# Two slots in place of three in the rings of rounded weight panels, each panel split one panel ahead

## The reference, cut to what matters

```python
# first_block, for each of 2 layers
y = rms_norm(x, in_norm_g) @ w_in + b_in          # then mLSTM, HGRN2 and a sliding-window attention
x = x + concat(m_out, h_out, s_out) @ w_out
x = x + square(relu(rms_norm(x, mlp_norm_g) @ w_up)) @ w_down          # width 4096
gate = sigmoid(rms_norm(x, ple_norm_g) @ w_ple_gate)
e = rms_norm(p @ w_ple_proj, ple_post_norm_g)
x = x + gate * e

# second_block, for each of 2 layers; mod is a product of the conditioning c
h = rmsnorm(x, g_attn) * (1 + scale1) + shift1
x = x + gate1 * mixer_layer(h)                    # w_in, three attentions, w_out
h = rmsnorm(x, g_mlp) * (1 + scale2) + shift2
u, g = split(h @ w_up)                            # width 2816 each
x = x + gate2 * ((silu(conv(g)) * u) @ w_down)
# after both: rmsnorm(x, g_final)
```

## Time and profile before

| what | value |
|---|---|
| median of 3 runs | 3312.72 us (3269.17 to 3331.93) |
| the profiled execution, its own time | 3291.14 us |
| its span, first to last instruction | 3289.3 us |
| its mean granted TensorE clock | 0.911 |
| TensorE busy | 2956.2 us, 90% of the span |
| TensorE weight loads busy | 2410.1 us, 73% |
| VectorE busy | 1736.4 us, 53% |
| ScalarE busy | 1126.6 us, 34% |
| remainders of panels (L308, VectorE) | 218 instructions, 469.5 us |
| roundings of panels (L296, ScalarE) | 218 instructions, 392.3 us |

### The profile page before, as it was taken

The page is one execution under the profiler, slowest core; times in us unless marked ns, Lnnn a source line. Parts: engine busy times, 40 slices in busy tenths (PEclk is TensorE's granted clock), DMA queues, the critical chain, the costliest instruction groups (busy, mean ns, idle before and its releaser), DMA issues. The chain is left out here.

```text
span 3289.3 us, 37690 instructions
## 1 busy us (share of the span) xinstructions
PE 2956.2 (90%) x14514; PEld 2410.1 (73%) x14514; DVE 1736.4 (53%) x2899; ACT 1126.6 (34%) x1851; POOL 197.9 (6%) x195
## 2 busy tenths in 40 slices
PE   5977889999879778899998699889999898989997
PEld 3957668888659576688886587768887687768886
DVE  4458356666654574555566554454352643454453
ACT  3251432222433515322234334433232434333232
POOL 1012010000200120100002000010001000010001
PEclk9955699999989558999999899999999899989999
DMA  4200024444132000244440311122321310122321
GB/s 162 98 13 1 1 70 160 167 168 154 69 116 90 13 1 14 91 160 164 161 166 32 129 64 32 35 77 87 112 82 53 125 63 28 44 73 77 120 87 61
DMA packets 42992, 281.35 MB, mean 86 GB/s; under 512 B 5944, under 2 KB 6200, under 8 KB 11704
## 3 DMA queue, kind: packets, MB, share of 16 engines
q1 hardware_dynamic: 42808, 278.86, 24.2%
HBM read 276.75 MB, written 2.10 MB: 85 GB/s over the span
## 5 line engine op out<-in xcount | busy, mean ns | idle before, releaser
L308 DVE TENSOR_TENSOR low_panels<-raw_panels,high_panels 128x2048 fp32r<-128x2048 f32 (+3 forms) x218 | 469.5, 2153 | 357.8 <-ACT high_panels L296 357.7
L296 ACT ACTIVATE high_panels<-raw_panels 128x2048 fp32r<-128x2048 f32 (+3 forms) x218 | 392.3, 1801 | 525.6 <-PE bank L1347 196.7
L409 PE MATMUL bank<-mlp_h_high,high_panels 128*128 128x512 f32 x1216 | 485.2, 399 | 37.8 <-DVE mlp_h_low L399 19.0
L409 PE MATMUL bank<-mlp_h_low,high_panels 128*128 128x512 f32 x1216 | 479.4, 394 | 0.0
L409 PE MATMUL bank<-mlp_h_high,low_panels 128*128 128x512 f32 x1216 | 479.2, 394 | 0.0
L409 PEld LDWEIGHTS bank<-mlp_h_high,high_panels 128*128 128x128 f32 x1216 | 230.1, 189 | 103.0 <-issue 36.8
L409 PEld LDWEIGHTS bank<-mlp_h_high,low_panels 128*128 128x128 f32 x1216 | 230.1, 189 | 51.6
L409 PEld LDWEIGHTS bank<-mlp_h_low,high_panels 128*128 128x128 f32 x1216 | 230.5, 190 | 48.1
L1347 PE MATMUL bank<-mlp_hid_high,high_panels 128*128 128x512 f32 x512 | 204.9, 400 | 0.0
L1347 PE MATMUL bank<-mlp_hid_low,high_panels 128*128 128x512 f32 x512 | 202.9, 396 | 0.0
L1347 PE MATMUL bank<-mlp_hid_high,low_panels 128*128 128x512 f32 x512 | 202.9, 396 | 0.0
(11 more groups left out here) (355 smaller groups left out, 5835.3 us busy)
## 6 DMA issues: line engine op xcount, KB each, us to landing
raw_panels<-in_w SPq DMA_DIRECT2D x238, 1024.0 KB, 4.9
raw_panels<-in_w SPq DMA_DIRECT2D x16, 384.0 KB, 3.2
raw_panels<-in_w SPq DMA_DIRECT2D x4, 960.0 KB, 4.6
raw_panels<-in_w SPq DMA_DIRECT2D x4, 768.0 KB, 4.1
row<-in_row SPq DMA_DIRECT2D x2, 1476.0 KB
x<-in_xT SPq DMA_DIRECT2D x1, 2048.0 KB, 7.5
raw_panels<-in_w SPq DMA_DIRECT2D x4, 512.0 KB, 7.6
mix<-in_rope SPq DMA_DIRECT2D x2, 1024.0 KB, 8.5
```

Source lines behind the costliest of these rows:

```text
L296: self.nc.scalar.activation(self.g.high[:, i % SPLIT, 0:raw.shape[1]], raw, ACT.Copy).then_inc(self.high_ready, 1)
L308: self.nc.vector.tensor_tensor(self.g.low[:, i % SPLIT, 0:w], raw, self.g.high[:, i % SPLIT, 0:w].bitcast(F32), ALU.subtract).then_inc(sel ...
L409: ins = nc.tensor.matmul(bank[:, :], w[a][:, k, c0:c0 + P], rhs[b][:, k0 + k, :], start=first and k == 0 and j == 0, stop=last and k == kt ...
```

## The change

`SPLIT` goes from 3 to 2 and `AHEAD` from 2 to 1. The second split inside the norm is taken out of the two input stages, since the panel loop that follows now begins with panel 1. In `embedding_gate` the list is written anew: panel first + 1, the first gate panel, is now split there and no longer at the end of the MLP, and the panels after it two output chunks later than their predecessors were.

```diff
-SPLIT = 3
-AHEAD = 2
+SPLIT = 2
+AHEAD = 1
...
-                    norm_scalar(nc, act, g, e, hh, before={0: lambda: pan.high(act, 0), 3: lambda: pan.high(act, 1)})
+                    norm_scalar(nc, act, g, e, hh, before={0: lambda: pan.high(act, 0)})
...
-                                before={1: lambda: pan.low(dve, 0), 4: lambda: pan.low(dve, 1)})
+                                before={1: lambda: pan.low(dve, 0)})
...
-                pan.high(act, first + 2)
-                pan.high(act, first + 3, full, DC)
+                pan.high(act, first + 1)
                 for c in range(DC):
-                    if c == 2:
-                        pan.high(act, first + 4, full, DC + 2)
+                    if c in (0, 2, 4):
+                        pan.high(act, first + 2 + c // 2, full, DC + c)
                     act.wait_ge(full, DC + c + 1)
...
                 norm_vector(nc, dve, g, e, x, vec[:, V_GPLE:V_GPLE + DC], hh, hl, before={0: p_low})
+                pan.low(dve, first + 1)
                 pan.low(dve, first + 2)
                 dve.wait_ge(ee.root_ready, 1)
                 st.link(nc.vector.reciprocal(erstd[:, 1, :], erstd[:, 0, :]))
-                pan.low(dve, first + 3)
                 for c in range(DC):
-                    if c == 2:
-                        pan.low(dve, first + 4)
+                    if c in (2, 4):
+                        pan.low(dve, first + 2 + c // 2)
...
-                norm_scalar(nc, act, g, e, hh, mod[:, 0:DC], {0: lambda: pan.high(act, 0), 3: lambda: pan.high(act, 1)}, s("shifts_ready"))
+                norm_scalar(nc, act, g, e, hh, mod[:, 0:DC], {0: lambda: pan.high(act, 0)}, s("shifts_ready"))
...
-                            {1: lambda: pan.low(dve, 0), 4: lambda: pan.low(dve, 1)})
+                            {1: lambda: pan.low(dve, 0)})
```

## The result

| | before | after |
|---|---|---|
| median | 3309.98 us (20 runs, 3269.17 to 3332.68) | 3330.61 us (20 runs, 3308.64 to 3351.05) |
| ratio, 95% interval | | 1.0109 (1.0087 to 1.0130) |
| profiled execution: time, span, granted clock | 3291.14 us, 3289.3 us, 0.911 | 3331.29 us, 3329.5 us, 0.903 |

The kernel is slower, by less than 2%. The ratio sets aside eight of the 20 runs of the kernel before, those over 1.5% above its fastest, and none of the kernel after, so it stands above the 1.0062 of the two medians (20.6 us).

A forecast was written before the change was run, and what follows sets the result against it. TensorE, busy 90% of the span, was taken as the bound, with splits hidden over long stretches. Terms summing to +25.0 us on a base of 3301.9 gave 3327 us, 0.75% slower, range 3283 to 3368.

The forecast's parts named there:

- the two bases: Starting times for the forecast: the profiled execution, 3291.14 us, and the median of the runs, 3312.72; their middle 3301.9 was taken.
- the sum: All terms over the whole kernel: 19.4 + 8.1 - 1.9 - 1.8 + 1.2 = +25.0 us.
- Full panels: In mlp_one and other stages with full panels, splits stay covered, 3.4 us early in modulated panels; costed at nothing.
- The embedding gate: First gate panel is split only after the embedding and norm, so TensorE waits; +9.7 us per layer, +19.4 in all.
- The lower bound of 7.9 us: Embedding gate: least cost per layer, if the first 24 matmuls ran at full clock.
- Short panels: w_down panels of 4.08 us can't cover a 4.58 us split; +0.6 us, 14 times, +8.1 in all.
- Second output panels: Second part: a smaller panel is split before the update of x, shortening TensorE's wait; -0.95 us per layer, -1.9 in all.
- Input norms: One remainder and its wait leave VectorE's list in each of four norms; -0.45 us each, -1.8 in all.
- The value panel: Second part: the split of panel 3 ends after TensorE wants it; +0.6 us per layer, +1.2 in all.
- Raw panels arriving late: Rival: in 48 modulated mlp_one panels, landings beyond 13.1 us cost 48 us per microsecond; slower by over 2%; chance 0.08.
- Addresses: Rival: operands moved by smaller rings change the matmuls' pace in the first part, 28 us less, 3299; chance 0.04.
- Two slots enough everywhere: Rival: gate panel's split covered and short panels just fit, so only the gains remain, 3298 us, not slower; chance 0.10.

The follow-up runs named there:

- e8: Changed kernel plus 36 unused matmuls per layer on TensorE while it waits for the first gate panel; 3316.26 us, ratio 1.0062 to the kernel before.
- e2: Changed kernel with every split made in two halves, each on ScalarE and then VectorE; 3330.71 us, ratio 1.0111 to the kernel before.
- e3: Changed kernel with three slots in the rings again, each panel still split one panel ahead; 3335.25 us, ratio 1.0143 to the kernel before.
- e5: Changed kernel with the ring of raw panels also cut from three slots to two; 3328.21 us, ratio 1.0092 to the kernel before.
- e4: Changed kernel with the first gate panel split at the MLP's end and every split in two halves; 3293.52 us, ratio 1.0011 to the kernel before.
- e6: Changed kernel with one extra remainder on VectorE ahead of each remainder in mlp_one; 3335.53 us, ratio 1.0101 to the kernel before.
- e10: The same kernel as e4, run again in more rounds; 3294.45 us, ratio 0.9986 to the kernel before.

## Why the prediction came out as it did

The kernel was forecast a little slower and is. 3327 us lies 3.6 below the median measured, and well inside the range. But as a change it was too small: the forecast stands 14.3 us, 0.43%, above the 3312.72 shown, and the ratio measured is 1.0109.

**The step that failed** is the last: "I take the middle of the two bases, 3301.9". It took 10.8 us off the base and so off the change against the median shown. On the median shown the same sum would have been 3337.7, or +0.75%. A base below the median that the change is measured against takes the difference out of the change, whatever the sum is worth; what the runs showed in its place is the four windows' +28.9 us, near the +25.0 of the sum. As a time the base stays in doubt: the kernel before had medians of 3300.53, 3302.09 and 3302.42 us in the three sets of runs beside the experiments, but 3309.98 in the 20 beside the changed kernel. With 28.9 the one leads to 3330.8 and the other to 3338.9. That 3327 came within 3.6 us of the median is in part luck: the base lay 8.1 below 3309.98, and the sum 4.4 above the medians' difference.

**The sum**, +25.0 us, was near, each large term slightly small:

- Full panels, nothing: right. `mlp_one` keeps 374.2 us. In the changed kernel a remainder there ends at 517.62, while the panel before it runs to about 521.0 (two evictions, at 509.59 and 521.27, with the remainder between):

```profile
509.59 0.60 ACT L1381 ACTIVATE mlp_relu<-bank 128x512 f32<-128x512 f32 x1 [4.50 <-PE bank L409]
...
515.34 2.28 DVE L308 TENSOR_TENSOR low_panels<-raw_panels,high_panels 128x2048 fp32r<-128x2048 f32 x1
...
521.27 0.60 ACT L1381 ACTIVATE mlp_relu<-bank 128x512 f32<-128x512 f32 x1 [4.50 <-PE bank L409]
```

- The embedding gate, +9.7 per layer: +10.0 and +10.2, by the steps named. The 24 matmuls took 8.0 us, not 7.4, because the granted clock over them was lower than in the row I took (0.68, and 0.74 in the earlier trace rows). The lower bound of 7.9 us "at full clock" is e8's 73.0 - 65.2 = 7.8.
- Short panels, +0.58 each, +8.1: +0.58 at the one shown, +8.7 in the windows. e2 takes all of it back.
- Second output panels, -0.95 per layer: the step happened and something else came of it. The two short waits are gone, 6.7 to 4.5 us. But TensorE now waits among the attention steps, at 2134.85:

```profile
2129.19 1.80 ACT L296 ACTIVATE high_panels<-raw_panels 128x1920 fp32r<-128x1920 f32 x1
...
2131.03 2.16 DVE L308 TENSOR_TENSOR low_panels<-raw_panels,high_panels 128x1920 fp32r<-128x1920 f32 x1 [2.60 <-ACT high_panels L296]
...
2134.85 1.13 PE L1791 MATMUL bank<-q_and_k 64*128 64x256 f32 x8 [1.58 <-DVE stats L2003]
```

  VectorE waits 2.60 us for a rounding, makes the remainder, and only then takes the maxima that free TensorE's bank. I had looked at who waits for the moved remainder and not at what is queued behind it. The statistics' waits grew by 1.4 us, so by the list of waits 0.8 us of the 2.2 were kept; what that is as time was not taken apart.
- Input norms, -1.8: not shown. TensorE's waits at L423 fell from 40.5 + 36.9 to 39.7 + 36.1, that is by 1.6, but in e8, with the same lists there, they are 39.8 + 37.4, and in e3 39.4 + 35.9: they scatter by as much.
- The value panel, +0.6 per layer: not seen. The stretch from the norm to the first attention wait went from 179.0 us to 178.4 and 178.5.
- Raw panels arriving late: didn't happen, and e5 shows that a whole slot less is hidden as well. Addresses: e3, nothing. Two slots enough everywhere: false as the lists stood, true once the panel is split early and in halves. There the rule of the Trainium skill, page "Trainium Kernel Development and Optimization", section "Best Practices", to double-buffer for performance, which the page gives for overlapping transfers with compute, holds for these rings as well: the trace of e4 agrees, with 65.1 and 363.7 us in place of 75.2 and 368.0.
- Two slips in the working: the lower end of the output panels, -5.1, comes to -4.5 from its rows (2 by 0.96 and 2 by 1.3), and -0.45 for an input norm lies on the worse side of its bounds' middle, -0.7. Neither moves the sum by more than 1 us.

**The total.** The windows make 28.9 us, the medians 20.6, and the ratio's interval 29 to 43 us on the 3295 that 3330.61 / 1.0109 gives. The spans of the two profiled executions differ by 40.2 us, but 7.0 of them lie in one stretch of the first layer's attention, before and after:

```profile
322.70:404.90 82.20, 79.35 (x319) 0.61 0.00 1
```

```profile
322.50:411.70 89.20, 86.87 (x319) 0.54 0.00 1
```

The last section shows that this stretch varies within one kernel; in the second layer it takes 67.3 us in both traces. Without the two stretches the span is 3139.8 us before, and 3173.0, 3167.1, 3173.0 and 3166.8 us in the changed kernel, e3, e5 and e6, whose windows are the same: 27.0 to 33.2 us more, with 28.9 among them. The kernel of e4 and e10 has 3135.9 and 3141.0. So outside these stretches the change costs 27 to 33 us, of which the windows show 28.9. Where the few us beyond lie stays open, and there is one trace of the kernel before.

## What to carry to other kernels

A ring's size and its lead are two things: here the third slot was worth nothing without the second panel of lead, and the two together 29 us in the windows. For a lead of one, compare the latency of making the next operand with the shortest unit of work ahead of it, and look for places where nothing runs ahead at all, such as a stage's first panel. Such places can be mended one by one, by doing the work in the stage before or by passing it on in halves, and then the smaller ring cost nothing that 22 runs could tell: 8 KiB per partition saved in each of the two rings.

## What the runs showed of the hardware that was not expected

**VectorE beside GpSimd.** In e2 a remainder of half a panel took 1.96 us while GpSimd added, and 1.23 alone. The Trainium skill, page "SBUF — State Buffer", section "SBUF: two separate sides", says that VectorE and GpSimd share a pair of ports as an exclusive lock, and that a VectorE instruction with two inputs in on-chip memory waits for a GpSimd one that reads it and began first. The trace agrees: the half starts at 888.18, GpSimd's addition ends at 889.06, and the half ends 1.08 us later. A half that starts at 451.82, 0.40 us before GpSimd ends an addition, takes 1.47 us and ends 1.07 us after it.

**One stretch, several lengths.** The last stretch of the first part's attention, the same 319 or 320 matmuls, takes from 67.3 to 91.7 us, and both within one execution of one kernel. TensorE over it in the two layers of e4:

```profile
322.30:389.60 67.30, 63.97 (x319) 0.81 0.00 1
1210.00:1301.70 91.70, 89.45 (x320) 0.52 0.00 1
```

The granted clock is 0.81 in one and 0.52 in the other. The kernel before shows 82.2 us at 0.61 and 67.3 at 0.81 in its two layers. Some 24 us in each of two layers would make 49 of the 63 us by which its runs differ; that is argued, and what decides the clock there was not tried.
